# First block of a two-block transformer kernel: rotated query parts scaled in one piece and moved by transfers, norm factors in other PSUM banks, first head's keys and values ahead of the rest

## The reference, cut to what matters

```python
q = (rms_norm(q_lat, g_q_lat[l]) @ w_q_b[l]).reshape(B, S, MLA_HEADS, MLA_NOPE + MLA_ROPE)
q_nope = rms_norm(q[..., :MLA_NOPE], g_mla_q_nope[l])
q_pe = rope(rms_norm(q[..., MLA_NOPE:], g_mla_q_pe[l]), positions)
kv = (rms_norm(kv_lat, g_kv_lat[l]) @ w_kv_b[l]).reshape(B, S, MLA_HEADS, MLA_NOPE + MLA_V)
k_nope = rms_norm(kv[..., :MLA_NOPE], g_mla_k_nope[l])
v_mla = kv[..., MLA_NOPE:]
k_pe = rope(rms_norm(k_pe, g_mla_k_pe[l])[:, :, None, :], positions)
k_mla = jnp.concatenate([k_nope, jnp.broadcast_to(k_pe, (B, S, MLA_HEADS, MLA_ROPE))], axis=-1)
q_mla = jnp.concatenate([q_nope, q_pe], axis=-1)
o_mla = causal_dense_attention(q_mla, k_mla, v_mla, (MLA_NOPE + MLA_ROPE) ** -0.5)
```

## Time and profile before

| what | value |
|---|---|
| median of 3 runs | 2587.87 us (2584.29 to 2588.84) |
| the profiled execution's own time | 2584.02 us |
| span of its trace | 2582.7 us |
| PE busy | 98% of the span |
| DVE, ACT, POOL busy | 48%, 37%, 7% |
| mean granted TensorE clock | 0.996 of full speed |
| HBM traffic | 103 GB/s over the span |

### The profile page before, as it was taken

The page is one execution under the profiler, slowest core; times in us unless marked ns, Lnnn a source line. Parts: engine busy times, 40 slices in busy tenths (PEclk is TensorE's granted clock), DMA queues, the critical chain, the costliest instruction groups (busy, mean ns, idle before and its releaser), DMA issues.

```text
span 2582.7 us, 27632 instructions
## 1 busy us (share of the span) xinstructions
PE 2535.3 (98%) x11505; PEld 2054.3 (80%) x11505; DVE 1242.3 (48%) x1773; ACT 954.5 (37%) x1296; POOL 170.9 (7%) x172
## 2 busy tenths in 40 slices
PE   8989999999999999999999999999999999999998
PEld 5667778888888888878788888888888777888886
DVE  6686656664343333356743333433333466533333
ACT  5456543343232222336532222322222355422221
POOL 1111000000001110000011100011100000011100
PEclk9999999999999999999999999999999999999999
DMA  7433213332322223321222223322222322222231
GB/s 284 146 106 116 69 66 115 130 114 98 100 103 93 98 96 114 114 98 62 86 98 98 98 98 101 112 98 98 97 100 98 119 70 89 89 94 97 96 114 65
DMA packets 41390, 267.20 MB, mean 103 GB/s; under 512 B 5449, under 2 KB 5833, under 8 KB 11698
## 3 DMA queue, kind: packets, MB, share of 16 engines
q1 hardware_dynamic: 37440, 256.92, 28.9%
q0 software_dynamic: 2576, 7.10, 0.9%
q10 hardware_dynamic: 1250, 1.42, 0.2%
HBM read 262.78 MB, written 4.21 MB: 103 GB/s over the span
## 4 chain that ended last, share of the span: by engine, by line
PE 94%; DVE 3%; ACT 2%; issue 1%; DMA 0%; ACTq 0%; DVEq 0%
PE ps L412 29%; PE ps L414 29%; PE ps L413 29%; PE ps L960 1%; PE ps L708 1%; ACT tmp L1316 1%; PE ps L994 1%; PE ps L691 0%; DVE wlo L1647 0%; PE ps L580 0%; PE ps L664 0%; PE ps L981 0%; PE ps L582 0%; PE ps L581 0%; PE ps L451 0%
## 5 line engine op out<-in xcount | busy, mean ns | idle before, releaser
L1647 DVE TENSOR_TENSOR wlo<-raw,whi 128x2048 fp32r<-128x2048 f32 x213 | 488.1, 2292 | 1066.7 <-ACT whi L1132 1066.6
L412 PE MATMUL ps<-ahi,whi 128*128 128x512 f32 x2272 | 896.8, 395 | 1.3 <-ACT tmp L1316 1.3
L414 PE MATMUL ps<-alo,whi 128*128 128x512 f32 x2272 | 886.1, 390 | 0.0
L413 PE MATMUL ps<-ahi,wlo 128*128 128x512 f32 x2272 | 885.7, 390 | 0.0
L1132 ACT ACTIVATE whi<-raw 128x2048 fp32r<-128x2048 f32 x213 | 407.8, 1915 | 885.6 <-PE ps L414 882.6
L412 PEld LDWEIGHTS ps<-ahi,whi 128*128 128x128 f32 x2272 | 427.5, 188 | 95.5 <-issue 7.8
L414 PEld LDWEIGHTS ps<-alo,whi 128*128 128x128 f32 x2272 | 427.4, 188 | 90.3
L413 PEld LDWEIGHTS ps<-ahi,wlo 128*128 128x128 f32 x2272 | 427.7, 188 | 89.2 <-issue 2.6
L412 PE MATMUL ps<-hhi,whi 128*128 128x512 f32 x1008 | 393.1, 390 | 3.3 <-DVE hhi L2287 3.3
L413 PE MATMUL ps<-hhi,wlo 128*128 128x512 f32 x1008 | 392.2, 389 | 0.0
L414 PE MATMUL ps<-hlo,whi 128*128 128x512 f32 x880 | 342.3, 389 | 0.0
(11 more groups left out here) (389 smaller groups left out, 1715.4 us busy)
## 6 DMA issues: line engine op xcount, KB each, us to landing
raw<-wstream SPq DMA_DIRECT2D x221, 1024.0 KB, 4.8
raw<-wstream SPq DMA_DIRECT2D x24, 512.0 KB, 5.0
early<-ada_in SPq DMA_DIRECT2D x8, 1024.0 KB, 20.4
strip<-bias_strips POOLq DMA_DIRECT2D x16, 256.0 KB, 4.1
x<-x_in SPq DMA_DIRECT2D x2, 1024.0 KB, 6.7
bias_strips<-bias_by_distance POOLq DMA_DIRECT2D x1, 2048.0 KB, 16.6
y_out<-x SPq DMA_DIRECT2D x3, 512.0 KB, 2.7
bd<-lru_in ACTq DMA_DIRECT2D x2, 256.0 KB, 3.4
```

Source lines behind the costliest of these rows:

```text
L412: pe.matmul(out, wh, rhi, start=start, stop=False)
L413: pe.matmul(out, wl, rhi, start=False, stop=False)
L414: return pe.matmul(out, wh, rlo, start=False, stop=stop)
L1647: dve.tensor_tensor(lo_of(u)[:], raw[r][:], hi_of(u)[:].bitcast(F32), ALU.subtract).then_inc(*inc("lo_dve", "lo", u))
```

## The change

The two rotated query parts are multiplied by their factors as whole tiles of 128 partitions into a new buffer `q_turned` (region 35.5, where `kv_lo` and later `E` lie), and eight transfers issued by SP bring the 32 partitions of each head to partitions 64 to 95 of `qt`. The copy of the rotated key to all heads goes from POOL's queue to SP's, behind these eight, and no longer stands in POOL's program. `head_scores(0)` and `head_scores(4)` wait for the four transfers of their half. The factors of `qn` 3, `qp` 0, `qp` 1 go to banks 3, 5 and 4 right behind those of `qn` 1 and 2, and those of `kn` 0, `rms` and `kn` 1 to banks 0, 3 and 5; z tile 1 goes to bank 7. The statistics of z tiles 0 and 1 and the factors of `kn` 2 and 3 move behind the scores and values of head 0. On DVE, `kn` 0 and the values of heads 0 and 1 come ahead of `sine(("z", 0))` and `split(8)`; the other values and keys come behind `head_top(0)`.

```diff
@@ head_scores @@
                 pe.wait_ge(*at("k_pe"))
+                if h % 4 == 0:
+                    pe.wait_ge(*at("q_pe", h // 4))
...
@@ PE, behind the projections @@
+            scale(("qn", 3), 3, ("r", "q"))
+            scale(("qp", 0), 5, ("tile", ("v", 2)))
+            scale(("qp", 1), 4, ("tile", ("v", 3)))
             z_half(0, 0, 6, ("sin", ("qp", 1)))
-            scale(("qn", 3), 0, ("head", ("qn", 1)))
-            scale(("qp", 0), 1, ("head", ("qn", 2)))
             z_half(0, 1, 6)
-            scale(("qp", 1), 0, ("head", ("qn", 3)))
-            statistics(("z", 0))
-            scale("rms", 1, ("head", ("qp", 0)))
-            scale(("kn", 0), 3)
-            z_half(1, 0, 6, ("moved", ("z", 0)))
-            scale(("kn", 1), 5, ("tile", ("v", 2)))
-            z_half(1, 1, 6)
-            scale(("kn", 2), 3, ("head", ("kn", 0)))
-            scale(("kn", 3), 5, ("head", ("kn", 1)))
-            head_scores(0, ("values_ok", 3), ("head", ("qp", 1)))
-            statistics(("z", 1))
-            head_values(0)
+            scale(("kn", 0), 0, ("head", ("qn", 1)))
+            z_half(1, 0, 7, ("sin", ("qp", 0)))
+            scale("rms", 3, ("head", ("qn", 3)))
+            scale(("kn", 1), 5, ("head", ("qp", 0)))
+            z_half(1, 1, 7)
+            head_scores(0, ("head", ("qn", 2)), ("r", "kv"))
+            head_values(0, ("head", ("qp", 1)))
             for h in range(8):
-                z_half(h + 2, 0, 6, ("moved", ("z", h + 1)) if h < 7 else ("tile", ("z", 8)))
+                z_half(h + 2, 0, 6, ("moved", ("z", h + 1 if h else 0)) if h < 7 else ("tile", ("z", 8)))
+                if h == 0:
+                    pe.wait_ge(*at("moved", ("z", 1)))
+                    statistics(("z", 0))
+                    statistics(("z", 1))
+                    scale(("kn", 2), 3, ("values_ok", 3))
...
                 z_half(h + 2, 1, 6)
+                if h == 0:
+                    scale(("kn", 3), 5, ("head", ("kn", 1)))
@@ ACT @@
+            split(8)
             z_out(0, 6)
-            split(8)
-            z_out(1, 6)
+            z_out(1, 7)
@@ DVE, head @@
                 elif t[0] == "qp":
                     dve.wait_ge(*at("roped", t))
-                    for i in range(4):
-                        w = slice(32 * i, 32 * i + 32)
-                        ins = dve.tensor_tensor(qt[64:96, 4 * t[1] + i, :], tile[w], ps[w, b, :], ALU.mult)
+                    ins = dve.tensor_tensor(q_turned[:, t[1], :], tile, bank(b), ALU.mult)
@@ POOL @@
-            pool.wait_ge(*at("head", ("qp", 1)))
-            pool.dma_start(kt_[64:96, :, :], kpe[64:96, :].unsqueeze(1).broadcast_to([32, 8, S]))
@@ SP @@
                 load(v)
+                if STREAM[v] == UNITS[8]:
+                    for n in range(2):
+                        sp.wait_ge(*at("head", ("qp", n)))
+                        for i in range(4):
+                            ins = sp.dma_start(qt[64:96, 4 * n + i, :], q_turned[32 * i:32 * i + 32, n, :])
+                    sp.dma_start(kt_[64:96, :, :], kpe[64:96, :].unsqueeze(1).broadcast_to([32, 8, S]))
```

More of the change, by code:

```diff
@@ L250, in build @@
         qt, kt_ = region("qt", 9, [P, 8, S]), region("kt", 17, [P, 8, S])
+        q_turned = region("q_turned", 35.5, [P, 2, S])
         mla_out = [(region(f"mla_hi{i}", 9 + 2 * i, [P, S], F32R), region(f"mla_lo{i}", 10 + 2 * i, [P, S], F32R)) for i in range(4)]
@@ L665, in pair_scores, with head_values @@
                 ins.then_inc(*inc("scores", "pair_scores", p, step))
-            def head_values(h):
+            def head_values(h, *free):
+                for step in free:
+                    pe.wait_ge(*at(*step))
                 pe.wait_ge(*(at("values_ok", h // 2) if h < 8 else at("tile", ("z", 8 + (h - 8) // 2))))
@@ L1971, in dve_program, with values_ok @@
             head(("qn", 2), 1)
-            head(("qn", 3), 0)
-            head(("qp", 0), 1)
-            head(("qp", 1), 0)
-            sine(("z", 0))
[L1976 to L1980, removed]
+            head(("qn", 3), 3)
+            head(("qp", 0), 5)
+            head(("qp", 1), 4)
+            head(("kn", 0), 0)
+            def values_ok(i):
+                dve.wait_ge(*at("scale", "rms"))
+                dve.wait_ge(*at("tile", ("v", i)))
+                dve.tensor_tensor(vt[:, i, :], vt[:, i, :], bank(3), ALU.mult).then_inc(*inc("values_ok", "values_ok", i))
+            values_ok(0)
+            sine(("z", 0))
             split(8)
-            head(("kn", 1), 5)
-            head(("kn", 2), 3)
-            head(("kn", 3), 5)
             def head_top(h):
@@ L2056, in dve_program @@
             head_top(0)
+            for i in range(1, 4):
+                values_ok(i)
+            head(("kn", 1), 5)
             sine(("z", 1))
+            head(("kn", 2), 3)
+            head(("kn", 3), 5)
             ada_acc(11)
@@ L2493, in pool_program @@
                 rotate(t)
-            pool.wait_ge(*at("head", ("qp", 1)))
-            pool.dma_start(kt_[64:96, :, :], kpe[64:96, :].unsqueeze(1).broadcast_to([32, 8, S])).then_inc(*land("d_kpe", "k_pe"))
             for j in range(8):
@@ L2569, in sp_program @@
                 load(v)
+                if STREAM[v] == UNITS[8]:
[3 more added lines that the diff above has]
+                            ins = sp.dma_start(qt[64:96, 4 * n + i, :], q_turned[32 * i:32 * i + 32, n, :])
+                            ins.then_inc(*land(f"d_qpe{n}", *(("q_pe", n) if i == 3 else ("q_pe_part", n, i))))
+                    sp.dma_start(kt_[64:96, :, :], kpe[64:96, :].unsqueeze(1).broadcast_to([32, 8, S])).then_inc(*land("d_kpe", "k_pe"))
             for j, n in ((0, 2), (2, 2), (4, 2), (6, 1), (7, 1)):
```

## The result

The change is slower by a little: 2590.68 us in the median of 20 runs (2587.74 to 2592.41) against 2585.67 for 20 runs of the kernel before (2581.20 to 2588.95), a ratio of 1.0016 with a 95% interval of 1.0009 to 1.0022 (the two medians alone give 1.0019). Run again on another chip beside three of the experiments it gave 1.0011 (1.0002 to 1.0020). The profiled execution took 2589.62 us, its span is 2588.3.

What follows compares the result with a forecast made beforehand. PE, 98% busy, was taken as the bound, with a load chain behind DVE's unit 11 limiting gains; ACT's 1.69 us lead shrinks by 0.9, leaving -0.8: 2587.87 - 0.8 = 2587.1 us, range 2583.5 to 2591.5.

Steps and rivals of the forecast that it cites:

- Four waits go, one comes at head 0's scores, released by a DMA: PE before head 0's scores: old waits totalling 7.83 us go, a new one of 4.2 us comes; scores start 5.9 earlier.
- Eight products become two, DVE saves 4.3 us: DVE, rotated query parts: 5.66 us become 1.4 on 128 partitions; the saving does not reach modulation unit 11.
- Two loads in a row took 0.80 us, 0.40 each, so the ninth is issued at 137.5: SP's queue: nine transfers issued 0.40 us apart from 134.3, the rotated key's copy last, at 137.5.
- The bound of 0.74: SP's queue: issues 0.74 us apart put the ninth at 140.2 and its landing at 144.9, making the change +1.9 us.
- The 4.7 us for the landing: Rotated key's copy: 4.7 us from issue to landing, as on POOL's queue, so head 0's scores start at 142.2.
- The step that failed: DVE's key 3: factors ready at 152.7, behind PE's 10 us from the scores' start; unit 11 at 154.2, 0.9 later.
- the maxima began 2.36 us after the start of scores: DVE, head 0: row maxima follow the scores' start by 2.36 us, as in head 2, so begin at 144.6.
- Rival C: Head 2: PE's clock falls to the lower level after idling, adding 2.9 us, 2590.0 us; chance 0.12.
- What is late next: unit 11, load, split, z tile 3, ACT's lead of 1.69: Chain behind unit 11 shifts 0.9 us; ACT's lead over PE at z tile 3 shrinks to 0.8, the gain left.
- Rival B: Rotated key's copy moves only after the other eight land: lands at 146.9, 3.9 us slower, 2591.8 us; chance 0.18.
- Rival A: PE keeps its 5.9 us lead from head 0's scores, 2582.0 us; unit 11's earliest start limits gain to 5.0; chance 0.1.

Runs made afterwards that it cites:

- e12: The change itself run again, unedited, on another chip beside three experiments; 2590.56 us, 1.0011 of the kernel before.
- e2: The change with 26 matmuls that nobody reads put into PE's wait ahead of head 0's scores; 2586.64 us, 0.9997 of the kernel before.
- e10: The change with the rotated key's copy in two halves, heads 0 to 3 first, unit 11 still behind key 3; 2578.61 us, 0.9967 of the kernel before.
- e3: The change with modulation unit 11 put on DVE ahead of head 0's row maxima; 2579.24 us, 0.9968 of the kernel before.
- e7: The change with the key copy in two halves and modulation unit 11 ahead of head 0's row maxima; 2575.08 us, 0.9955 of the kernel before.
- e5: The change with the rotated key's copy issued by SP as the fifth transfer instead of the ninth; 2587.23 us, 0.9999 of the kernel before.
- e8: The change with the last three values, key 1 and z tile 1's sine back ahead of head 0's maxima on DVE; 2589.23 us, 1.0010 of before.

## Why the prediction was wrong

It forecast a gain of 0.8 us and "the same"; measured are +5.0 us (+3.0 on the other chip) and, beyond the interval, a loss, though one below the 0.2% it counted as no change and inside its range, 2583.5 to 2591.5. That it lies inside is partly luck: the forecast was built on a median of 2587.87 from three runs, and 20 runs gave 2585.67. With that median the forecast would have been 2584.9 and the range would have ended at 2589.3, below the measured 2590.68.

- *Four waits go, one comes at head 0's scores, released by a DMA*: right. PE was ready where it should have been: behind D, the forecast was 138.0 - 130.54 = 7.5, measured 135.6 - 128.02 = 7.6.
- *Eight products become two, DVE saves 4.3 us*: right, 1.29 us for both. That DVE's saving would not reach unit 11 was right too.
- *"Two loads in a row took 0.80 us, 0.40 each, so the ninth is issued at 137.5"*: the first term that was mis-sized. Each issue took 0.63 us. The ninth came at D + 8.88 instead of D + 6.96, which is 1.9 of the 2.3 us by which the scores were later than forecast. The bound of 0.74 covered it. The 4.7 us for the landing were right (4.8), and the Trainium skill's formula (DMA: Bandwidth & Descriptors, Anatomy of one DMA), 3.2 us here, was off on SP's queue as it was on POOL's. Its rule against many small transfers (same page, Rules for kernel authors) spoke rightly against the change, but the cost lay in issuing them, not in moving them: each landed in 2.0 us.
- *The step that failed*: "Key 3 needs factors that PE makes behind the scores, ... 10 us after the scores' start", and with it "the maxima began 2.36 us after the start of scores". Both price PE's work behind the new wait at full speed, although the forecast itself let PE stand still for 4 us there. It waited 6.34, its clock fell while it stood still, the scores took 4.6 us, and the maxima began 4.64 behind their start. From the start of the scores to unit 11 the forecast had 12.0 us (154.2 - 142.2). The change took 15.3, and e12 14.4; e2 and e10, where the clock was up at the scores, both took 12.1. So the sum was right for a PE at full speed and short by 3.3 us for the lower clock, and key 3's wait for PE (1.50 us on DVE) shows that PE's work was what unit 11 waited for. Unit 11 came at D + 29.2 instead of D + 23.7: of these 5.6 us, 2.3 are the late scores' and 3.3 the lower clock's. Rival C had the clock fall, but only in head 2, as something on top.
- *What is late next: unit 11, load, split, z tile 3, ACT's lead of 1.69*: right, and e3 shows it. Unit 12 comes 5.4 us later, the split 5.2, and 5.2 - 1.69 = 3.5 is what the last turn of head 1 lost, 51.24 - 47.88 = 3.4. One sign of it was missing: ACT's split did not wait for its load but followed head 1's exponentials without a gap, and these hang on unit 12 as well, over head 1's maxima.
- *Rival C*: came true as well, twice as long as priced: 16 us of clock 0.50 in head 1's end and head 2, which took the loss from 3.4 to 8.1 us in the profiled execution. In e12's profile that stretch lies where PE waits anyway and costs nothing there (3.9 us at the last turn and at the mix).
- *Rival B*'s time, 2591.8, is close, but for another reason: nothing waited for the eight to land; they were slow to be issued.
- *Rival A*: the change could not keep PE's lead, but the ceiling of 5.0 us that I put on it holds only while unit 11 stays where it is. With it moved and the key split, 12 us were there.

## What to carry to other kernels

A wait removed from the busiest engine is worth what the next limit leaves over; here that was a chain of loads, each freed by the work of a slower engine, and a piece of that engine's program that needs nothing new (modulation unit 11) should stand in its idle time, not behind a wait. Where small transfers replace vector work, price the issuing engine's time for each, and put the one transfer that the next step needs first, in a part no larger than that step needs. Waits of PE of 3.0 to 6.4 us were mostly paid twice in this kernel, once as idle time and once at the lower clock behind it; but the one of 3.18 us in e7 was not, and the clock fell behind shorter ones too (1.89 us in the change).

## What the runs showed that I had not expected

A transfer from SBUF to SBUF of 32 rows of 2 KB took SP 0.63 us to issue, against 0.40 for a load of 1 MB, and 0.91 while POOL had the copy of the key under way (7.31 us for eight); the copy's landing went from 4.8 to 5.6 us then. A second queue is not needed for this: in e5, with all on SP's queue, the issues behind the copy took 1.06 us each. Behind half of the copy, in e10, they took 0.65. Why the issuing slows down is not shown.

The time of an execution follows its mean granted clock. Of the 64 runs of the kernel before made beside the experiments, 40 had 0.995 (mean time 2588.1), 13 had 0.996 (2586.5) and 11 had 0.997 (2584.0). The execution whose trace the prediction rests on had 0.996 and 2584.02 us, less than any of the 13 (2585.6 to 2587.9) and among the 11 with 0.997 (2582.7 to 2585.4). So the 3.85 us between it and the median, which I carried along as a constant, are mostly the difference between a quick execution and a usual one; which stretch runs low in the others I can't say, since they left no trace. The change had 0.993 or 0.994 in 16 of 20 runs. So much of the loss of the change, and part of the gains against it, goes with PE time at 1.2 GHz: e7, 12 us faster, had 0.997 to 0.999. Waits do not explain all such time: the nearest wait of PE ahead of before's stretch is one of 0.77 us, and behind the last turn of head 1 e8 has a stretch from 182 to 189 us after a wait of 1.49 us, while e12 has none there after 1.58.
